# Most of the modulation moved into the first FFN, one opening stage, and a last norm by diagonal matmuls

## What is computed

```python
mod = silu(c) @ w_mod + b_mod                       # per stream, 9 blocks of 1024 values
sh1, sc1, g1, sh2, sc2, g2, sh3, sc3, g3 = split(mod, 9)
h = rmsnorm(x, norm_g[0]) * (1 + sc1) + sh1
x = x + 0.5 * g1 * swiglu(h, gate[0], up[0], down[0])
h = rmsnorm(x, norm_g[1]) * (1 + sc2) + sh2
x = x + g2 * mixer(h)
h = rmsnorm(x, norm_g[2]) * (1 + sc3) + sh3
x = x + 0.5 * g3 * swiglu(h, gate[1], up[1], down[1])
y = rmsnorm(x, final_norm)
```

## Time and profile before

| | us |
|---|---|
| median of 3 runs | 2903.91 (2902.78 to 2904.89) |
| the profiled execution | 2906.12 |
| its span | 2904.3 |
| TensorE busy | 2659.8 (92%) |
| VectorE busy | 1352.2 (47%) |
| ScalarE busy | 702.4 (24%) |
| mean granted clock of TensorE | 0.942 |
| stages: x loaded and turned / modulation / first FFN begins | 22.4 / 129.6 / 130.9 |
| second FFN ends / output stage begins / last copy ends | 2870.0 / 2871.6 / 2900.4 |

### The profile page before, as it was taken

One profiled execution on the slowest core, in us unless ns is written; L12 is line 12 of the kernel. 1 busy time (PEld: TensorE's weight loads), 2 busy tenths in 40 slices (PEclk: granted clock), 3 DMA queues, 4 the chain that ended last, 5 costly groups with the idle time before them and its releaser, 6 DMA issues. The chain is left out here.

```text
span 2904.3 us, 51209 instructions
## 1 busy us (share of the span) xinstructions
PE 2659.8 (92%) x21152; PEld 2501.5 (86%) x21152; DVE 1352.2 (47%) x2671; ACT 702.4 (24%) x1341; POOL 87.1 (3%) x158
## 2 busy tenths in 40 slices
PE   5699999999999799976979797869999999999997
PEld 2299999999999799944868677669999999999996
DVE  3263333333333866316385857443633333333336
ACT  2131111111111411115344444221411111111112
POOL 0000000000000000000021120200000000000000
PEclk7699999999999999986889898979999999999998
DMA  8721111111110122142221212051211111111101
GB/s 338 285 64 44 36 43 43 43 36 43 43 43 8 29 92 92 47 179 80 55 45 57 63 40 63 13 182 32 71 41 40 43 44 43 43 38 34 43 22 66
DMA packets 213164, 193.77 MB, mean 67 GB/s; under 512 B 63859, under 2 KB 183454, under 8 KB 213022
## 3 DMA queue, kind: packets, MB, share of 16 engines
q1 hardware_dynamic: 212752, 191.65, 20.4%
q10 hardware_dynamic: 270, 0.09, 0.0%
HBM read 159.01 MB, written 32.70 MB: 66 GB/s over the span
## 5 line engine op out<-in xcount | busy, mean ns | idle before, releaser
L129 PE MATMUL ff_ps<-h_hi,ff_wlo 128*128 128x384 f32 x2112 | 708.7, 336 | 8.5 <-DVE ff_wlo L624 5.5
L131 PE MATMUL ff_ps<-h_hi,ff_whi 128*128 128x384 f32 x2112 | 708.2, 335 | 0.0
L130 PE MATMUL ff_ps<-h_lo,ff_whi 128*128 128x384 f32 x2112 | 708.2, 335 | 0.0
L631 DVE TENSOR_TENSOR ff_s<-ff_ps,ff_s 128x384 f32<-128x384 f32 x132 | 73.6, 557 | 730.9 <-PE ff_ps L131 728.7
L129 PEld LDWEIGHTS ff_ps<-h_hi,ff_wlo 128*128 128x128 f32 x2112 | 398.2, 189 | 11.1 <-DVE ff_wlo L624 6.0
L131 PEld LDWEIGHTS ff_ps<-h_hi,ff_whi 128*128 128x128 f32 x2112 | 398.4, 189 | 0.0
L130 PEld LDWEIGHTS ff_ps<-h_lo,ff_whi 128*128 128x128 f32 x2112 | 398.2, 189 | 0.0
L129 PE MATMUL ff_ps<-ff_uhi,ff_wlo 128*128 128x384 f32 x1056 | 352.9, 334 | 0.0
L130 PE MATMUL ff_ps<-ff_ulo,ff_whi 128*128 128x384 f32 x1056 | 352.7, 334 | 0.0
L131 PE MATMUL ff_ps<-ff_uhi,ff_whi 128*128 128x384 f32 x1056 | 352.7, 334 | 0.0
L579 ACT ACTIVATE ff_s<-ff_ps 128x384 f32<-128x384 f32 x132 | 64.9, 492 | 753.3 <-PE ff_ps L131 753.3
(11 more groups left out here) (289 smaller groups left out, 3193.9 us busy)
## 6 DMA issues: line engine op xcount, KB each, us to landing
md_w<-w_mod SPq DMA_DIRECT2D x9, 4096.0 KB, 24.2
ff_raw<-ffn_w_gate SPq DMA_DIRECT2D x44, 512.0 KB, 4.7
ff_raw<-ffn_w_up SPq DMA_DIRECT2D x44, 512.0 KB, 4.0
ff_raw<-ffn_w_down SPq DMA_DIRECT2D x44, 512.0 KB, 3.5
pj_raw<-w_in SPq DMA_DIRECT2D x19, 512.0 KB, 4.1
z_dram<-pj_zo SPq DMA_DIRECT2D x15, 576.0 KB, 3.0
rw_rkv<-z_dram SPq DMA_DIRECT2D x12, 576.0 KB, 7.0
x_dram<-x SPq DMA_DIRECT2D x1, 4608.0 KB, 21.3
```

Source lines behind the costliest of these rows:

```text
L129: pe.matmul(out, w_lo, x_hi, start=start, stop=False)
L130: pe.matmul(out, w_hi, x_lo, start=False, stop=False)
L131: return pe.matmul(out, w_hi, x_hi, start=False, stop=stop)
L631: dve.tensor_tensor(hid[:, t % 2, :], ps[:, 2 + t % 2, 0:CW], silu[:, t % 2, :], ALU.mult)\
```

## The change

1. `load_stage` and `mod_stage` become one `open_stage`. SyncE queues three blocks of `w_mod` (0 to 2) right behind x. The turning of x uses four PSUM banks instead of six. Squares, additions and sums of the root mean squares follow the copies directly. The silu of c is made first and also kept in `cs`. Only these three blocks are made by matmuls.
2. The other six blocks (6144 columns) are made in the first FFN, by a new class `Modulation`, 768 columns in each of groups 1 to 8. ScalarE issues eight transfers of 128x768 a group (384 KB, into the unused `ff_n`); VectorE multiplies each by c and c_ctx and accumulates (16 operations a group: one pair behind each of the six hidden tiles and behind updates 11 and 19); at a group's end TensorE sums over partitions by 12 one-column matmuls into bank 7, and VectorE keeps the result in `mod`. Group 9 then stands outside the loop. After group 8 `finish_modulation` adds bias and gains.
3. Since bank 7 is taken, the down tiles of the first FFN go through three banks (`DB`); the second FFN keeps four.
4. `out_stage` has no `Norm` and no y: TensorE multiplies x's 128x128 pieces with diagonal matrices of `final_norm` (72 plain matmuls, which turn and scale at once) through eight banks, the copies out of PSUM multiply with `inv`, now one value a partition, and nine row buffers take the result.

```diff
+def open_stage(nc, io, sb):
...
+                for j in range(W):
+                    sp.dma_start(w[:, j, :, :], wsrc[:, :, j * D:(j + 1) * D]).then_inc(w_in[j], 16)
...
+                for c in range(NC):
+                    stats.sum(pe, c)
+                for j in range(W):
+                    pe.wait_ge(w_in[j], 16)
...
+class Modulation:
+    COLS, BLOCKS = 768, 8
...
+    def load(self, act, g, k):
+        if k:
+            act.wait_ge(self.used, g * (2 * KD) + (2 * k - 2 * KD))
+        else:
+            act.wait_ge(self.kept, g)
+        act.dma_start(self.w, self.src[:, k, bass.ds(g * self.COLS + (NMOD // 3 * D - self.COLS), self.COLS)]).then_inc(self.w_in, 16)
+
+    def slice(self, dve, g, k):
+        dve.wait_ge(self.w_in, g * (16 * KD) + (16 * (k + 1) - 16 * KD))
+        if k:
+            dve.wait_ge(self.used, g * (2 * KD) + (2 * k - 2 * KD))
+        for s in range(2):
+            c, acc = self.sb["cs"][:, k, s:s + 1], self.acc[:, s, :]
+            if k:
+                dve.scalar_tensor_tensor(acc, self.w, c, acc, ALU.mult, ALU.add).then_inc(self.used, 1)
+            else:
+                dve.tensor_scalar(acc, self.w, c, None, ALU.mult).then_inc(self.used, 1)
+
+    def sum(self, pe, g):
+        pe.wait_ge(self.used, g * (2 * KD))
+        pe.wait_ge(self.kept, g)
+        for j in range(self.COLS // P):
+            for s in range(2):
+                last = pe.matmul(self.ps[:, 2 * j + s:2 * j + s + 1], self.acc[:, s, j * P:(j + 1) * P],
+                                 self.sb["cst"][:, C_ONE:C_ONE + 1], start=True, stop=True)
...
 def ffn_stage(nc, io, sb, f, h_hi, h_lo):
...
+        DB = 4 if f else 3
+        rest = None if f else Modulation(st, io, sb, tmp[:, :, :], ps[:, 7, :])
...
-                            last = mm3(pe, ps[:, 4 + n % 4, 0:CW], w_hi[:, D0 + m, os], w_lo[:, D0 + m, os],
+                            last = mm3(pe, ps[:, 4 + n % DB, 0:CW], w_hi[:, D0 + m, os], w_lo[:, D0 + m, os],
...
+                if rest:
+                    with pe.Fori(1, rest.BLOCKS + 1) as g:
+                        group(g, False)
+                        rest.sum(pe, g)
...
                         hidden(g, t)
+                        if rest:
+                            rest.slice(dve, g, t)
...
+                        if n in (11, 19) and rest:
+                            rest.slice(dve, g, TILES + (n == 19))
...
+def out_stage(nc, io, sb):
...
-                        last = pe.transpose(ps[:, n % 4, k * P:(k + 1) * P], y[:, half * 4 + k, t * P:(t + 1) * P],
-                                            sb["cst"][:, C_ID:C_ID + P])
+                        last = pe.matmul(ps[:, n % RING, k * P:(k + 1) * P], sb["x"][:, half * 4 + k, t * P:(t + 1) * P],
+                                         gain[:, half * 4 + k, :], start=True, stop=True)
```

More of the change, by code:

```diff
@@ L216, in _ @@
                         sb["x"][:, half * 4:half * 4 + 4, t * P:(t + 1) * P],
[L217 to L282, removed]
@@ new lines, in _, with finish_modulation @@
+                dve_t.wait(dve, f"mod{W - 1}")
+                finish_modulation(dve, sb, dve_t, range(1))
+def finish_modulation(dve, sb, steps, norms):
+    mod, at = sb["mod"], PRM["norm_g"][0]
+    part = slice(norms[0] * 3 * KD, (norms[-1] + 1) * 3 * KD)
+    mv = mod[:, part, :].rearrange("p (i m k) s -> p i m (k s)", m=3, k=KD)
+    steps.did("b", dve.tensor_tensor(mod[:, part, :], mod[:, part, :],
+                                     sb["bmod"][:, part].unsqueeze(2).to_broadcast([P, part.stop - part.start, 2]), ALU.add))
+    steps.wait(dve, "b")
+    steps.did("sc", dve.tensor_scalar(mv[:, :, 1, :], mv[:, :, 1, :], 1.0, None, ALU.add))
+    steps.wait(dve, "sc")
+    for i in norms:
+        m = mod[:, (3 * i + 1) * KD:(3 * i + 2) * KD, :]
+        last = dve.tensor_tensor(m, m, sb["prm"][:, at + i * KD:at + (i + 1) * KD].unsqueeze(2).to_broadcast([P, KD, 2]), ALU.mult)
+    steps.did("g", last)
+    gate = mod[:, (3 * norms[-1] + 2) * KD:(3 * norms[-1] + 3) * KD, :]
+    steps.did("h", dve.tensor_scalar(gate, gate, 0.5, None, ALU.mult))
@@ L608, in _ @@
                 group(0, opening=True)
-                with act.Fori(1, GROUPS - 1) as g:
+                if rest:
+                    with act.Fori(1, rest.BLOCKS + 1) as g:
+                        group(g, rest=rest)
+                with act.Fori(1 if rest is None else rest.BLOCKS + 1, GROUPS - 1) as g:
                     group(g)
@@ L674, in _ @@
                 group(0, opening=True)
-                with dve.Fori(1, GROUPS - 1) as g:
+                if rest:
+                    dve.sem_inc(rest.kept, 1)
+                    with dve.Fori(1, rest.BLOCKS + 1) as g:
+                        group(g, rest=rest)
+                        rest.keep(dve, g)
+                    rest.finish(dve)
+                with dve.Fori(1 if rest is None else rest.BLOCKS + 1, GROUPS - 1) as g:
                     group(g)
@@ new lines, in _ @@
+                for half in range(2):
+                    ks = slice(half * 4, half * 4 + 4)
+                    dve.tensor_tensor(gain[:, ks, :], ident.unsqueeze(1).to_broadcast([P, 4, P]),
+                                      sb["prm"][:, at + half * 4:at + half * 4 + 4].unsqueeze(2).to_broadcast([P, 4, P]),
+                                      ALU.mult).then_inc(gains, 1)
+                for t in range(NT):
+                    dve.wait_ge(turned, 2 * t + 1)
+                    dve.tensor_scalar(rows[:, t, 0:512], ps[:, 2 * t % RING, :], sb["inv"][:, t:t + 1], None, ALU.mult)\
+                       .then_inc(copied[0], 1)
```

230 lines of the change are left out of this document (127 added, 103 removed).

## The result

| | before | with the change |
|---|---|---|
| median, same chip | 2904.4 us (4 runs, 2902.8 to 2917.2) | 2873.5 us (4 runs, 2871.0 to 2891.7) |
| ratio, 95% interval | | 0.9887 [0.9853, 0.992] |
| profiled execution / span | 2906.12 / 2904.3 | 2874.92 / 2873.1 |

The account below looks back on a forecast made before the run. TensorE, busy 2659.8 of 2904.3 us, was taken to bound the kernel, with transfers binding the opening. Opening 71.7, first FFN -31.2 and output stage 11.3 sum to 51.8 us less, 2852.1 us; range 2843 to 2872.

Parts of the forecast that it names:

- The opening: Opening stage, bound by transfers: with six blocks gone it ends at 57.9 instead of 129.6 us, a gain of 71.7 us.
- First FFN, item 1, the sums: End of each first-FFN group: 12 one-column matmuls, 24 records at 0.097 us, add 2.3 us a group.
- Items 2 and 3, the ring and the late slices: First-FFN down tiles: three banks make TensorE stand 1.2 us; slices behind tiles 11 and 19 cost 0.05 and 0.3 us.
- What hides under TensorE: First FFN: transfers, ScalarE's issue, VectorE's products in the tile part, keep and finish cost nothing.
- The clock: First FFN: granted clock stays 1.00; the rival, falls at the new stalls, gives 2865 to 2878 us, chance 0.17.
- The output stage: Output stage: 72 plain matmuls, 144 records, 17 at 0.22 and 127 at 0.097 us; gain 11.3 us.
- The four-turn rival: Output stage: a plain FP32 matmul costs four turns, so the stage ends 7 us later; result 2870 us, chance 0.03.
- Late slices: First FFN: slice transfers landing steadily above 8.4 us make it slower, about 3003 us; 0.03 together with an unchanged opening.
- the blocks delay x: Opening: mixed transfers complete x only at 43 us, so the opening ends 22 us later; 2874 us, chance 0.06.
- The sum: Whole kernel: 71.7 - 31.2 + 11.3 = 51.8 us less, a median of 2852.1 us; chance 0.70.
- one fall a group: First FFN: one clock fall a group at 1.6 us each costs 13 us, giving 2865; clock rival's chance 0.17.

Follow-up runs that it names:

- merge_only: Against the changed kernel, all nine w_mod blocks are made in the merged opening through three slots, first FFN as before the change; 2883.1 us, ratio 0.9893 to before.
- comb: Changed kernel with four down-tile banks, products ahead of hidden tiles, last pairs behind updates 5 and 12, two sums behind each of down tiles 17 to 22; 2849.2 us.
- best: Changed kernel with the edits of comb and out_turn together; 2849.2 us, ratio 0.9798 to before.
- one_sum: Changed kernel with one 12-column matmul in place of the twelve one-column matmuls at a group's end, blocks 3 to 8 not computed; 2856.4 us.
- comb_end: Changed kernel with four down-tile banks, products ahead of hidden tiles, last pairs behind updates 5 and 12, the twelve sums together at the group's end; 2861.8 us.
- out_turn: Changed kernel with 72 transposes in the output stage; VectorE, ScalarE and GpSimd apply inv and gain afterwards; 2874.9 us, ratio 0.9907 to before.

## Why the prediction was right, and where not

*The opening* was right, in size and in reason: 72.1 us against 71.7, the first block at the forecast time, the limit now the engines. merge_only adds what the prediction had not split: 10 us are the joined stage's, 62 the removed transfers'.

*First FFN, item 1, the sums*: mis-sized. A record took 0.108 us where I had 0.097 from the earlier trace rows; 2.6 us a group for 2.3, so 2.4 us in eight. The row I read was the end of a burst of 128-column matmuls beside a change of shape, too short a stretch (six records) to price 192. The trace of before had the right one, at full clock (granted 1.00 from 2022 to 2026), and I overlooked it:

```profile
2023.41 2.14 PE L359 MATMUL op_ps<-cst,op_s 128*128 128x1 f32 x18 [1.39 <-DVE op_s L354]
```

Its 18 one-column records start 0.111 us apart, which would have given 2.7 us a group.

*Items 2 and 3, the ring and the late slices*: the mechanism and the tiles were right (1.1 us idle at tile 3, 0.2 at tile 23), the price was not. The products take 0.97, not 0.9; tiles 3, 15 and 23 cost 1.42, 0.24 and 0.5 us, against 1.2, 0.05 and 0.3: 17.3 us for 12.4. I had priced the standing and left out that the first matmul behind a wait is followed 0.12 us late.

*What hides under TensorE* (transfers, ScalarE's issue, the other products, `keep`) cost nothing, as said: in comb and best the stage is longer than before by the sums alone.

*The clock* was the step that failed. I gave one fall a group a chance of 0.17 and kept PEclk at 1.00 because at 1006 us the clock had stood through short waits. That row was about waits, and about waits it told the truth (one_sum). It told nothing of 2.6 us of one-column matmuls without a gap. The one burst of them at full clock in the trace of before, the row above, could not have settled it: the clock fell at 2026.29, 2.9 us after the burst began, but TensorE had had nothing to do since 2025.55. The price of one fall, 1.6 us from the earlier trace rows, was right. Six give 9.6 us. With 2.4 and 4.9 from the other items that is 16.9, against 15.9 us by which the stage missed. So the terms add up to one us too much; each is a step read to a few hundredths and taken eight times.

*The output stage*: the mechanism was right, 7.7 us came for 11.3. Half clock lasted until 2855, 5 us instead of 17 records at 0.22 (3.7 us), and a plain record at full clock was 0.112 for 0.097: the burst was 18.9 us where I had 16.1. The first product came 0.6 us later after `inv` than L419 had before, and `inv` itself 0.5 us later after the last update of x. The four-turn rival fell: at full clock a plain product takes two records, 0.224 us, and the burst of 72 is 2.0 times that of 72 turns (18.91 against 9.55 us), where I had 1.7. The factor of 4 that the Trainium skill gives for FP32 (TensorE: Matmul & The Clock Gate, Terms) is seen in no trace here. What I missed is that a turn would still have been the better choice.

*Late slices* and *the blocks delay x* did not occur: the slices land in 3.3 us, and the last tile of x lands at 17.0 us, where it had 16.6 before.

*The sum*: 2852 was forecast and 2873.5 came, just outside the upper end of 2872 as a median. By the ratio, 0.9887 of the 2903.91 before is 2871.1, just inside. That is no merit of the sum: the forecast gain was 52 us and 31 came, 16 of the missing ones in the first FFN and 4 in the output stage, and the range was wide because it took in the falls that the sum itself put at nothing. The rival "one fall a group" with 2865 would have been the nearer one.

## What to carry to other kernels

One-column sums can cost clock besides their own time (1.6 us a fall here): put them between wide matmuls, two at a time, not in one burst. Look for the price of a new kind of instruction in a long burst of it at the clock level where it will run, and count a wait with what follows it. Where most runs scatter in an untouched stage, compare stage lengths, and check there which engine got longer before believing a median.

## What was not expected of the hardware

- A burst of 24 one-column matmul records, 2.6 us at a granted clock of 1.00 with TensorE busy throughout, was followed by some ten matmuls at 0.50 in six of eight groups (in four of eight in comb_end). The same 24 records in six pieces of 0.5 us had no fall in eight groups, and that twice (comb, best). Why some groups are spared stays open; it is no pure chance, as after and out_turn spare the same two.
- The records of TensorE count it as busy (2.00 of 2 us) in the burst that precedes the fall, as in the wide matmuls before it.
- The trace shows one-column f32 matmuls 0.111 us a record at full clock, no faster than 128-column ones (0.112).
- The rwkv stretch varies by 22 us between executions of the same instructions, with the clock between 0.89 and 0.85.
